# First attention: the weights of the patch keys transposed by the DMA in 16-bit planes

## The reference

```python
h = concatenate([meta, x])                    # 272 tokens
hn = rms_norm(h, norm_mix[0])
c = hn @ mla_w_in                             # latents for q and for k, v, and a shared rope key
q = rms_norm(c_q) @ mla_w_uq                  # per head 128 plain + 64 turned columns
k, v = rms_norm(c_kv) @ mla_w_ukv             # per head 128 + 128 columns
s = (q_plain @ k_plain.T + rope(q_r) @ rope(k_r).T) * (128 + 64) ** -0.5 + mask
p = softmax(s)                                # float32, 272 x 272 per head
o = p @ v
h = h + o @ mla_w_o
```

## Time and profile before

| what | value |
|---|---|
| median of 3 runs | 3057.98 us (3057.9 to 3058.08) |
| profiled execution | 3058.66 us, its span 3056.9 us |
| PE busy | 3043.0 us (100%), 20906 matmuls |
| DVE busy | 1869.1 us (61%) |
| ACT busy | 1469.8 us (48%) |
| POOL busy | 134.2 us (4%) |
| mean granted TensorE clock | 0.999 |
| weights on SP's queue | 532.14 MB, 50.0% of 16 DMA engines |
| chain that ended last | PE 97%, DVE 1%, ACT 1%, DMA 1% |

### The profile page before, as it was taken

One profiled execution on the slowest core, in us unless ns is written; L12 is line 12 of the kernel. 1 busy time (PEld: TensorE's weight loads), 2 busy tenths in 40 slices (PEclk: granted clock), 3 DMA queues, 4 the chain that ended last, 5 costly groups with the idle time before them and its releaser, 6 DMA issues.

```text
span 3056.9 us, 48305 instructions
## 1 busy us (share of the span) xinstructions
PE 3043.0 (100%) x20906; PEld 2827.8 (93%) x20906; DVE 1869.1 (61%) x2263; ACT 1469.8 (48%) x1699; POOL 134.2 (4%) x132
## 2 busy tenths in 40 slices
PE   9999999999999999999999999999999999999999
PEld 9989999999999999989888888889998889999987
DVE  7775555445445557776565565556787666767663
ACT  5544433333333357755443443345565654555553
POOL 0001000000000011110000000002000001101000
PEclk9999999999999999999999999999999999999999
DMA  6334555555554554455555555554444545555554
GB/s 236 108 111 166 174 173 178 179 177 171 176 179 168 182 195 176 159 193 179 194 191 188 185 179 198 187 192 179 179 140 153 178 175 184 179 193 186 174 191 152
DMA packets 94516, 539.57 MB, mean 177 GB/s; under 512 B 25568, under 2 KB 26080, under 8 KB 31584
## 3 DMA queue, kind: packets, MB, share of 16 engines
q1 hardware_dynamic: 77264, 532.14, 50.0%
q10 hardware_dynamic: 17040, 4.34, 0.8%
HBM read 530.15 MB, written 2.10 MB: 174 GB/s over the span
## 4 chain that ended last, share of the span: by engine, by line
PE 97%; DVE 1%; ACT 1%; DMA 1%; issue 0%; SPq 0%; ACTq 0%; DVEq 0%
PE PB L1158 28%; PE PB L1159 15%; PE PB L1183 14%; PE PB L1182 14%; PE PB L1184 13%; PE PB L1177 2%; PE PB L1178 2%; PE PB L1179 2%; PE PB L1169 1%; PE PB L1168 1%; PE PB L1167 1%; PE PB L1240 1%; DMA raw<-in_mla_in 1%; PE PB L1308 1%; DVE WLt L1796 0%; PE PB L1309 0%
## 5 line engine op out<-in xcount | busy, mean ns | idle before, releaser
L1796 DVE TENSOR_TENSOR WLt<-raw,WHt 128x2048 fp32r<-128x2048 f32 (+2 forms) x506 | 1139.3, 2259 | 760.7 <-ACT WHt L1415 760.2
L1415 ACT ACTIVATE WHt<-raw 128x2048 fp32r<-128x2048 f32 (+2 forms) x506 | 955.0, 1890 | 1117.3 <-PE PB L1159 582.0
L1158 PE MATMUL PB<-Xt,WHt 128*128 128x512 f32 x2880 | 1027.6, 395 | 0.0
L1159 PE MATMUL PB<-Xt,WLt 128*128 128x256 f32 x2880 | 808.5, 281 | 0.0
L1158 PEld LDWEIGHTS PB<-Xt,WHt 128*128 128x128 f32 x2880 | 540.8, 188 | 109.8
L1182 PE MATMUL PB<-Xt,WHt 128*128 128x272 f32 (+1 forms) x2192 | 635.0, 290 | 2.8 <-DVE WLt L1796 1.9
L1183 PE MATMUL PB<-Xt,WHt 128*128 128x272 f32 (+1 forms) x2192 | 630.2, 287 | 0.0
L1184 PE MATMUL PB<-Xt,WLt 128*128 128x272 f32 (+1 forms) x2192 | 626.9, 286 | 0.0
L1159 PEld LDWEIGHTS PB<-Xt,WLt 128*128 128x128 f32 x2880 | 543.5, 189 | 0.1
L1182 PEld LDWEIGHTS PB<-Xt,WHt 128*128 128x128 f32 x2192 | 412.8, 188 | 12.6 <-DVE WLt L1796 4.9
L1183 PEld LDWEIGHTS PB<-Xt,WHt 128*128 128x128 f32 x2192 | 413.5, 189 | 1.1 <-issue 0.2
(11 more groups left out here) (268 smaller groups left out, 2858.1 us busy)
## 6 DMA issues: line engine op xcount, KB each, us to landing
raw<-in_gu SPq DMA_DIRECT2D x176, 1024.0 KB, 4.8
raw<-in_dn SPq DMA_DIRECT2D x88, 1024.0 KB, 4.8
raw<-in_odd_in SPq DMA_DIRECT2D x64, 1024.0 KB, 4.8
raw<-in_even_in SPq DMA_DIRECT2D x52, 1024.0 KB, 4.9
raw<-in_lru_in SPq DMA_DIRECT2D x24, 1024.0 KB, 4.9
raw<-in_mla_o SPq DMA_DIRECT2D x16, 1024.0 KB, 4.8
raw<-in_lru_o SPq DMA_DIRECT2D x16, 1024.0 KB, 5.0
raw<-in_even_o SPq DMA_DIRECT2D x16, 1024.0 KB, 4.9
```

The source lines that it names most:

```text
L1158: t.matmul(o, wh, both, start=first, stop=False)
L1159: m = t.matmul(o[:, 0, :], wl, ah, start=False, stop=last)
L1415: a.activation(hi, r, ACT.Copy).then_inc(s_hi, 1)
L1796: v.tensor_tensor(lo, r, hi.bitcast(f32), sub).then_inc(s_lo, 1)
```

## The change

The three 128 x 128 transposes of each head on PE and ACT's copy of them go, and with them bank `tr1`. In their place ACT copies the weights of the 256 patch keys apart into a plane of high and a plane of low 16-bit halves (four instructions, step `mla_planes`) and issues one transposing DMA. Its result is woven together by ACT (high halves) and DVE (low halves) in a step `mla_weave`, and `mla_pv` on PE waits for both. The planes use a buffer of the squares (`sqt`), the transposed planes two others by turns (`acct`, `tab`). The three transposes of the meta part stay.

```diff
     def transposes(hd):
-        p.take("tr1", hd)
         p.take("tr2", hd)
         p.mark("tr", "tr", hd)
-        p.give("tr1", hd)
         p.give("tr2", hd)
         p.step("mla_transposes", hd)
+
+    def mla_planes(hd):
+        p.mark("mla planes", "mla planes", hd)
+        p.step("mla_planes", hd)
+
+    def mla_weave(hd):
+        p.mark("mla woven", "mla woven", hd, 1)
+        p.mark("mla woven low", "mla woven", hd, 0)
+        p.step("mla_weave", hd)
...
         a, b = 2 * q, 2 * q + 1
+        p.inside(2, 1, lambda a=a: mla_weave(a))
+        p.inside(3, 1, lambda b=b: mla_weave(b))
         if q < 7:
-            p.after(0, lambda a=a, b=b: (scores(a), scores(b), normed_pair(a)))
-            p.after(1, lambda a=a, q=q: (transposes(a), q_rope(q + 1)))
+            p.after(0, lambda a=a, b=b: (scores(a), scores(b), normed_pair(a), mla_planes(a)))
+            p.after(1, lambda a=a, b=b, q=q: (transposes(a), mla_planes(b), q_rope(q + 1)))
...
+        MLA_PLANES, MLA_CROSSED = sqt[:, 0:384], (acct[:, 0:384], tab[:, 960:1344])
...
                 t.transpose(b2[0:16, 16:144], E[:, 0:16], ident)
-                t.transpose(b2[0:16, 144:272], E[:, 144:160], ident)
-                t.transpose(b1[:, 0:128], E[:, 16:144], ident)
-                t.transpose(b1[:, 128:256], E[:, 160:288], ident)
-                t.transpose(b1[:, 256:384], E[:, 288:416], ident).then_inc(sems["tr"], 1)
+                t.transpose(b2[0:16, 144:272], E[:, 144:160], ident).then_inc(sems["tr"], 1)
...
-                t.wait_ge(*when("out", "tr1", hd))
                 t.wait_ge(*when("out", "tr2", hd))
+                for i in range(2):
+                    t.wait_ge(*when("mla woven", hd, i))
...
+            def mla_planes(hd):
+                E, planes = Sm_[hd % 2], MLA_PLANES.bitcast(u16).rearrange("p (a n) -> p a n", a=2)
+                a.wait_ge(*when("p", hd))
+                if hd:
+                    a.wait_ge(s_mla_crossed, 16 * hd)
...
+                for i in range(2):
+                    a.activation(planes[:, i, 0:128], halfwords(E[:, 16:144])[:, i, :], ACT.Copy)
+                    m = a.activation(planes[:, i, 128:384], halfwords(E[:, 160:416])[:, i, :], ACT.Copy)
+                m.then_inc(sems["mla planes"], 1)
+                a.wait_ge(*when("mla planes", hd))
...
+                x = MLA_CROSSED[hd % 2].bitcast(u16).rearrange("p (g n) -> p g n", n=128)
+                a.dma_start(x, MLA_PLANES.bitcast(u16), transpose=True).then_inc(s_mla_crossed, 16)
+
+            def mla_weave(hd):
+                a.wait_ge(s_mla_crossed, 16 * (hd + 1))
                 if hd:
                     a.wait_ge(*when("pv", hd - 1))
-                a.activation(TT[:, 0:384], PB[b][:, 0:384], ACT.Copy).then_inc(s_bank[b], 1)
+                a.activation(halfwords(TT[:, 0:384])[:, 1, :], MLA_CROSSED[hd % 2].bitcast(u16)[:, 384:768],
+                             ACT.Copy).then_inc(sems["mla woven"], 1)
...
+            def mla_weave(hd):
+                v.wait_ge(s_mla_crossed, 16 * (hd + 1))
+                if hd:
+                    v.wait_ge(*when("pv", hd - 1))
+                v.tensor_copy(halfwords(TT[:, 0:384])[:, 0, :],
+                              MLA_CROSSED[hd % 2].bitcast(u16)[:, 0:384]).then_inc(sems["mla woven low"], 1)
```

More of the change, by code:

```diff
@@ L369, in make_plan @@
         else:
-            p.after(0, lambda a=a, b=b: (scores(a), scores(b), normed_pair(a)))
-            p.after(1, lambda a=a: transposes(a))
+            p.after(0, lambda a=a, b=b: (scores(a), scores(b), normed_pair(a), mla_planes(a)))
+            p.after(1, lambda a=a, b=b: (transposes(a), mla_planes(b)))
             p.after(2, lambda a=a, b=b: (pv(a), transposes(b)))
@@ L1029, in build_program @@
             ctx.enter_context(nc.semaphore(f"s_{n}")) for n in ("par", "cst", "lams", "tabA", "tabB", "last_gain", "out"))
+        s_mla_crossed = ctx.enter_context(nc.semaphore("s_mla_crossed"))
         s_crossed = ctx.enter_context(nc.semaphore("s_crossed"))
@@ L1098, in _ @@
                     s.wait_ge(*when("turned", 7))
+                    for i in range(2):
+                        s.wait_ge(*when("mla woven", 15, i))
                     s.dma_start(tab[:, :], A["tabB"]).then_inc(s_tabB, 16)
@@ L1244, in mla_transposes @@
                 E = Sm_[hd % 2]
-                b1 = own("tr1", hd)
                 b2 = own("tr2", hd)
@@ L1520, in mla_scores @@
                 e.then_inc(sems["ex"], 1)
-            def mla_transposes(hd):
-                b = plan.bank["tr1", hd][0]
-                a.wait_ge(*when("tr", hd))
+            def mla_planes(hd):
[3 more added lines that the diff above has]
+                    a.wait_ge(s_mla_crossed, 16 * hd)
+                else:
+                    a.wait_ge(*when("acc", ("c", 7)))
+                    a.wait_ge(*when("sum", "kv"))
+                for i in range(2):
+                    a.activation(planes[:, i, 0:128], halfwords(E[:, 16:144])[:, i, :], ACT.Copy)
+                    m = a.activation(planes[:, i, 128:384], halfwords(E[:, 160:416])[:, i, :], ACT.Copy)
+                m.then_inc(sems["mla planes"], 1)
+                a.wait_ge(*when("mla planes", hd))
+                if hd > 1:
+                    for i in range(2):
+                        a.wait_ge(*when("mla woven", hd - 2, i))
+                x = MLA_CROSSED[hd % 2].bitcast(u16).rearrange("p (g n) -> p g n", n=128)
+                a.dma_start(x, MLA_PLANES.bitcast(u16), transpose=True).then_inc(s_mla_crossed, 16)
+            def mla_weave(hd):
+                a.wait_ge(s_mla_crossed, 16 * (hd + 1))
                 if hd:
                     a.wait_ge(*when("pv", hd - 1))
-                a.activation(TT[:, 0:384], PB[b][:, 0:384], ACT.Copy).then_inc(s_bank[b], 1)
+                a.activation(halfwords(TT[:, 0:384])[:, 1, :], MLA_CROSSED[hd % 2].bitcast(u16)[:, 384:768],
+                             ACT.Copy).then_inc(sems["mla woven"], 1)
             def mla_pv(hd):
@@ L1739, in _ @@
                     mla_scores(*x)
-                elif what == "mla_transposes":
-                    mla_transposes(*x)
+                elif what == "mla_planes":
+                    mla_planes(*x)
+                elif what == "mla_weave":
+                    mla_weave(*x)
                 elif what == "mla_pv":
@@ L1955, in mla_scores @@
                     v.wait_ge(*when("tr", hd - 2))
+                    v.wait_ge(*when("mla planes", hd - 2))
                 for i, (n, x, y) in enumerate(blocks[:2]):
```

## The result

| | before | changed |
|---|---|---|
| median | 3058.03 us (6 runs, 3057.83 to 3058.40) | **3077.01 us** (6 runs, 3071.18 to 3088.08) |
| ratio to before, 95% interval | | 1.0065 [1.0053, 1.0077] |
| profiled execution | 3058.66 us, span 3056.9 | 3078.66 us, span 3076.5 |
| mean granted TensorE clock of a run | 0.999 in the profiled one | 0.997 in the profiled one, 0.999 in the two shortest, 0.994 in the longest |

Slower by 19.0 us, where +11.9 was forecast. The six runs of before lie within 0.6 us and those of the changed kernel within 17. The two shortest, 3071.2 us, are 13.2 above before. So there are two things to explain: a loss of 13 us that is always there, and one of 0 to 17 us that comes and goes.

What follows compares the result with a forecast made beforehand. PE, busy for the whole span, was taken as the bound. Waits for DVE's low-half copy, less the transposes and bank wait saved, summed pair by pair to +11.9 us: 3069.9 us, range 3066.5 to 3078 (8 in 10).

Steps and rivals of the forecast that it cites:

- what goes: First attention, PE: 48 transposes removed, 5.3 us, and a bank wait of 0.97 us gone; savings of 6.3 us.
- head b's weaving late: mla_pv of head b behind DVE's low part: nothing in middle pairs, +0.9 us in the seventh, +1.0 in the eighth.
- head a's weaving late: mla_pv of head a waits for DVE's low-half copy: +2.0 us first pair, +1.63 each middle pair, +2.2 sixth.
- the clock falls behind the waits: PE's granted clock below 1.00 in 76 to 250 us: named only as a sign of error, without time or chance.
- ACT: Plane copies of 1.2 to 1.6 us and issue of 1.25 cost nothing in middle pairs; first pair delays DVE 0.66 us.
- ACT as a second bound: Rival: slower plane copies make DVE wait for v_out, +9.5 us, 3079; longest issue instead about +5, 3075. Chance 0.14.
- A late landing: Rival: the transposing DMA lands after 6.5 us, delaying head b's planes and v_out; +15 us, 3085. Chance 0.06.
- The estimate made block by block: Transposing DMA at the skill's 1309 ns a block: six blocks need 7.9 us, time near 3095; no separate chance.
- DVE's place: DVE's low-half copy stands behind the unit's low part, so PE waits at mla_pv of head a; +1.63 us per middle pair.
- the sum: First attention's eight pairs added: +2.0, +6.5 for second to fifth, +2.2 sixth, then smaller terms; +11.9 us unrounded.

Runs made afterwards that it cites:

- both early: Changed kernel with both heads' weaving steps moved earlier, to the end of the preceding unit: 3051.79 us, ratio 0.9979 to the kernel before.
- a early: Changed kernel with only head a's weaving moved earlier, head b's left in place: 3055.48 us, ratio 0.9991 to the kernel before.
- Without the new path: Kernel before without the three 128 x 128 transposes a head and ACT's copy, nothing in their place: 3050.48 us, ratio 0.9974.

## Why the prediction was 7 us too low, and what of its mechanism held

"Slower" was right, and the median of 3077.0 lies inside the range up to 3078, but the number was 7 us too low. The experiments split the difference into terms that can be laid beside those of the prediction and of the expectations. All are differences of medians, or of the shortest run where the mean clock was 0.999. They come from runs on several chips, on which the kernel before had medians of 3057.97 to 3058.36, so the sum is 18.6 here and 19.0 on the chip of the result:

| term | forecast | measured | from |
|---|---|---|---|
| what goes (transposes, bank) | -6.3 | -6.6 | both early less before |
| head b's weaving late | +2.7 | +3.7 | a early less both early |
| head a's weaving late | +15.5 | +15.7 | 3071.2 less a early |
| the clock falls behind the waits | 0 | +5.8 (0 to 17) | median less 3071.2 |
| sum | **+11.9** | **+18.6** | 3077.0 against 3058.4 |

**What goes.** Right. Without the new path it is a little more in the stage, 6.9 us, because a wait that I had not counted went too: at 187.92 PE waited for DVE's L1982, and the distance between the two starts was 0.45 us there in place of 0.12.

**ACT.** Right in six pairs of seven. The four copies took 1.1 us (forecast 1.2 to 1.6), the median issue 1.23 and 1.26 us (1.25), the DMA landed after 2.7 us (2.7). `v_out` ended 4.8 us after PE's unit (from 135.25 + 0.12, a matmul's distance, to 139.77 + 0.38), against a forecast of 5.0 to 5.4 and a DVE that comes 5.5 us after it. In the first pair DVE waited for ACT, 0.68 us against a forecast of 0.66. But it waited in a middle pair too, the fifth, where the issue held ACT's queue for 2.34 us:

```profile
179.31 2.34 ACTq L1549 DMA_TRANSPOSE tab<-sqt  x1
...
182.15 0.41 DVE L1909 TENSOR_TENSOR S<-PB,S 16x256 f32<-16x256 f32 x1 [0.32 <-ACT S L1520]
```

PE's wait in that pair is 2.39 us and not 2.00. It is the same pair in all four profiles of the changed kernel, with issues of 2.2 to 2.3 us, 0.20 to 0.32 us of waiting on DVE and 2.27 to 2.39 on PE. This is the rival of ACT as a second bound, with the longest issue, but in one pair and for some 0.4 us only. A late landing did not happen (3.6 us at most). The estimate made block by block from the figure of the Trainium skill ("VectorE: DVE Perf Modes", "The three transpose paths"), 7.9 us, is nearly three times what the trace shows.

**DVE's place.** Right: a wait bound to PE's own end of unit, back in every pair (in the seventh for both heads, in the eighth for head b alone). The distance from one `mla_pv` of head a to the next is 20.44 us (143.84 to 164.28), against 18.64 before; the forecast was 1.63 us more, and it is 1.80. Two small sizes make the 0.17. From the end of the copy to PE's start it takes 0.21 us and not 0.1. And PE restarts more slowly than it goes on: from the first multiplication of `mla_pv` to the first transpose behind it are 1.27 us after a wait (143.84 to 145.11) and 1.20 in the kernel before. This comes back in nearly every pair and, with the fifth pair's 0.4, makes about 1.5 us over the eight (an estimate from the traces, pair by pair, without the falls); between the runs the distance from 11.9 to 13.2 is 1.3.

**The step that failed** is "the sum": it prices each wait at its own length, at a full clock throughout. The prediction names the falling clock among the things that would make it wrong, "since the new waits of about 2 us are longer than any that the trace shows there", but gives it no price, no chance among the rivals, and no room in the range, which ended at 3078 by other causes. That the median fell inside is luck. It was wrong to treat as a remark what is a term: in the profiles a fall costs 2.6 to 4.3 us, and with six such waits the median run pays 6 us and the unluckiest 17. It also works out a single number where the kernel has none: the changed kernel's time is a spread.

The Trainium skill ("TensorE: Matmul & The Clock Gate", "HAM oscillation — how this bites in real kernels") describes this pattern, a stream with periodic waits whose every restart runs slow, and advises an order of the loop that keeps TensorE from waiting. This case agrees that a wait can slow the restart, and that the kernel gains when PE doesn't wait, though here only two of the six long waits were followed by a fall in each profile. But the idle gaps for which it gives that warning are longer than those of 2.02 to 2.4 us that were enough here.

## What to carry to other kernels

A part of a step that is given to a second engine belongs in that engine's queue ahead of its next long instruction, not behind it. Here the same work, at the same cost, gives 3077 or 3052 us by its place alone; read the order of the engine that helps, and find what it is doing when the first engine comes.

On a TensorE that is never idle, price a new wait of 2 us or more at its length and a chance of some us on top (2.6 to 4.3 for each fall here), and state a range that is open upwards. Runs that spread where the kernel before didn't, with a mean clock a few thousandths lower, are its mark; filling the wait with dummy work tells in one run whether the clock is to blame.

## What the runs showed of the hardware

- TensorE's granted clock fell to its lower level behind single waits of 2.02 us and more in an otherwise full stream, by chance: waits of 2.02 and 2.04 us in the same execution, one with and one without. Behind waits of 2.94 to 3.21 us it fell in every profile here, five in all. Behind waits of up to 1.8 us no profile of this stage shows it.
- A fall lengthened the stretch behind the wait by 2.6 to 4.3 us.
- Eight to twelve dummy multiplications in the place of each wait kept the clock at 1.00 in the profiled run and made the kernel 6 us faster, 3070.64 against 3076.55 on the same chip.
- A transposing DMA of six blocks of 128 x 128 halfwords between tiles of SBUF landed in 2.7 us (median), the longest in 3.6 in the changed kernel and 4.4 with the waits filled. Its issue held ACT's queue for 1.23 us mostly, and for up to 2.3 us in the changed kernel and 2.7 where ACT weaves both halves. In the changed kernel's four profiles one long issue fell in the same pair each time; why is not shown.
